# Three turns of adding rows back, moved to between the halves of the next item's gate and up

## The reference

```python
for e in range(N_EXPERTS):                      # 32 experts, D_EXPERT = 512
    hdn = jax.nn.silu(xn @ w_gate[e]) * (xn @ w_up[e])
    out = out + combine[:, e:e + 1] * (hdn @ w_down[e])
return x + out.reshape(bsz, t, d)
```

## Time and profile before

| | |
|---|---|
| runs, us | 833.37, 835.3, 836.32; median 835.3 |
| the profiled execution, us | 835.14, of which span 833.4 |
| granted TensorE clock, mean | 0.979 |
| PE busy | 771.5 us, 93% |
| DVE, ACT, POOL busy | 429.3, 320.9, 262.5 us |
| matmuls of the item loop: gate and up L1718, down L1747, gather L1677, turns L1706 | 169.1, 94.2, 70.5, 52.9 us |
| chain that ended last | PE 59%, DMA 17%, DVE 12%, SyncE's queue 7% |
| DMA in the item loop | 422 GB/s, busy share about 1.0 |

### The profile page before, as it was taken

How to read it: one execution, slowest core, us unless ns; L and a number is a source line. 1 busy time by engine, 2 the same in 40 slices (tenths; PEclk the granted TensorE clock), 3 DMA queues, 4 the chain that set the end, 5 groups by cost and what they waited for, 6 DMA issues and landing times.

```text
span 833.4 us, 21585 instructions
## 1 busy us (share of the span) xinstructions
PE 771.5 (93%) x8619; PEld 589.2 (71%) x8620; DVE 429.3 (52%) x1168; ACT 320.9 (39%) x556; POOL 262.5 (31%) x134
## 2 busy tenths in 40 slices
PE   4999999999999999999999979999998879989964
PEld 4999999999999999875556545555555545545532
DVE  3156978899994334064443433444443334434424
ACT  5433767555335844162223222322332213323223
POOL 4846699978576778400000000000000000000001
PEclk9999999999999999999999988999999999999997
DMA  7734343424444835986899999999999999999993
GB/s 251 236 106 148 102 141 113 153 96 144 154 170 152 302 125 207 340 344 232 361 421 422 422 422 422 422 422 422 422 422 422 422 422 422 422 422 422 423 422 142
DMA packets 53943, 250.77 MB, mean 301 GB/s; under 512 B 6713, under 2 KB 6731, under 8 KB 29333
## 3 DMA queue, kind: packets, MB, share of 16 engines
q1 hardware_dynamic: 50496, 247.74, 75.2%
q10 hardware_dynamic: 3413, 2.58, 1.2%
HBM read 247.54 MB, written 2.76 MB: 300 GB/s over the span
## 4 chain that ended last, share of the span: by engine, by line
PE 59%; DMA 17%; DVE 12%; SPq 7%; ACT 2%; issue 2%; ACTq 1%; DVEq 0%
PE bank L1571 24%; DMA piece<-in_exp_w_up 16%; PE bank L1718 12%; DVE bank L1097 7%; PE bank L1747 6%; SPq L566 6%; PE bank L1677 4%; PE bank L1706 4%; PE bank L1569 4%; DVE sq L1159 1%; PE bank L1734 1%; PE bank L1684 1%; DMA stage<-in_norm_g 1%; ACT cvb L845 1%; ACT w_hi L763 0%
## 5 line engine op out<-in xcount | busy, mean ns | idle before, releaser
L633 POOL TENSOR_TENSOR w_lo<-raw,w_hi 128x2048 fp32r<-128x2048 f32 x39 | 180.4, 4629 | 62.3 <-ACT w_hi L763 62.2
L1718 PE MATMUL bank<-piece,xe 128*32 128x256 f32 x2816 | 169.1, 392 | 29.0 <-DMA piece<-in_exp_w_up 23.2
L1718 PEld LDWEIGHTS bank<-piece,xe 128*32 128x32 f32 x2816 | 97.1, 113 | 93.6 <-issue 42.9
L1571 PE MATMUL bank<-x_hi,w_hi 128*128 128x384 f32 x432 | 145.6, 337 | 0.3 <-DVE ua L1116 0.2
L1571 PE MATMUL bank<-x_hi,w_lo 128*128 128x384 f32 x432 | 144.6, 335 | 0.0
L1571 PE MATMUL bank<-x_lo,w_hi 128*128 128x384 f32 x432 | 144.6, 335 | 0.0
L694 POOL TENSOR_SCALAR n_out<-n_out,small 128x512 f32<-128x512 f32 x2 | 3.6, 1786 | 442.2 <-DVE small L1456 442.2
L1097 DVE SCALAR_TENSOR_TENSOR bank<-ub,vec,bank 128x256 f32<-128x256 f32 (+1 forms) x416 | 137.2, 418 | 0.0
L763 ACT ACTIVATE w_hi<-raw 128x2048 fp32r<-128x2048 f32 x39 | 74.8, 1919 | 74.8 <-PE bank L1571 71.2
L1747 PE MATMUL bank<-piece,hidT 128*32 128x256 f32 x1408 | 94.2, 384 | 5.5
L1416 DVE SCALAR_TENSOR_TENSOR silu_and_hid<-bank,few,silu_and_hid 64x256 f32<-64x256 f32 x44 | 21.5, 488 | 132.8 <-ACT silu_and_hid L953 132.8
(11 more groups left out here) (239 smaller groups left out, 1020.8 us busy)
## 6 DMA issues: line engine op xcount, KB each, us to landing
piece<-in_exp_w_down SPq DMA_DIRECT2D x64, 1024.0 KB, 26.7
piece<-in_exp_w_gate SPq DMA_DIRECT2D x64, 1024.0 KB, 26.2
piece<-in_exp_w_up SPq DMA_DIRECT2D x64, 1024.0 KB, 26.6
raw<-in_w_in SPq DMA_DIRECT2D x28, 1024.0 KB, 5.2
raw<-in_w_out_a SPq DMA_DIRECT2D x4, 1024.0 KB, 5.1
raw<-in_w_out_b SPq DMA_DIRECT2D x4, 1024.0 KB, 5.2
raw<-in_w_o SPq DMA_DIRECT2D x4, 1024.0 KB, 5.0
out<-n_out SPq DMA_DIRECT2D x6, 256.0 KB, 2.2
```

Of the source, the lines that this page charges most:

```text
L633: pool.tensor_tensor(w_lo[u % NW][:, :, :], raw[u % NW][:, :, :], w_hi[u % NW][:, :, :].bitcast(F32), ALU.subtract).then_inc(lo_ready, 1)
L1571: ins = pe.matmul(b, wp[:, k % UK, cols], xp[:, k, :], start=start, stop=stop)
L1718: last = pe.matmul(GU[q * T:(q + 1) * T, :], xe[:, k, :], wide(pairs[q // 2], k)[:, q % 2 * QE:(q % 2 + 1) * QE], start=(k == 0), stop=(k ...
```

## The change

All three turns of an item's addition now stand between the two halves of the next item's gate and up, with the waits that the first turn needs ahead of them. The wait for `y_ready` moves with them from in front of `gather()`. None is left behind the gather, behind the row transposes or between the halves of down. What a turn computes, the other engines' lists and SyncE's list are unchanged.

```diff
@@ item(), TensorE @@
                     last.then_inc(done, 1)
+                    if part == 0:
+                        pe.wait_ge(y_ready, i + 2)
+                        pe.wait_ge(back_ready, i + 1)
+                        for turn in range(NT):
+                            pe.wait_ge(combined, i * NT + (turn + 1))
+                            combine(turn)
 
                 pe.wait_ge(picked, i + 2)
-                pe.wait_ge(y_ready, i + 2)
                 gather()
-                pe.wait_ge(back_ready, i + 1)
-                pe.wait_ge(combined, i * NT + 1)
-                combine(0)
                 pe.wait_ge(consts, 11)
                 pe.wait_ge(hid_ready, i + 1)
...
                 turn_rows()
-                pe.wait_ge(combined, i * NT + 2)
-                combine(1)
                 pe.wait_ge(hidT_ready, i + 1)
...
                     last.then_inc(done, 1)
-                    if part == 0:
-                        pe.wait_ge(combined, i * NT + 3)
-                        combine(2)
```

## The result

The changed kernel took 841.29 us (median of its runs, 840.07 to 842.35) against 835.81 for the kernel before (833.37 to 836.54): ratio 1.0069, interval 1.0051 to 1.0087. It is slower by some 5.5 us; 843.0 was predicted. Its profiled execution took 842.35 us, with a span of 840.6 against 833.4.

The account below looks back on a forecast made before the run. Weights bound the kernel before, TensorE the changed one: item 0 (+1.9 us), 42 items of 9.99 and 7 boundaries of 1.0 end the last down 7.9 us later, so 835.14 + 7.9 = 843.0 us, range 837.0 to 848.5.

Parts of the forecast that it names:

- What bounds: Item loop: weights set the end before the change; TensorE has 36 us of slack, 0.82 us for each item.
- Removed and added: Each item on TensorE: 0.76 us removed at the turns' old places, 1.75 added between the halves; item 9.99 us.
- Item 0: First item of the loop: its turns wait for GpSimd's zeroing of back_to, so the next item starts 1.9 us later.
- Boundaries: Seven round boundaries in the item loop: each adds 1.0 us on TensorE, as in the kernel before.
- The stream of weights: SyncE's refills restart 3.9 us later; the last up piece lands at 815.6, 6.6 us before TensorE asks for it.
- The slow clock: Item loop: low clock follows waits for pieces and goes with them; some 9 us, part of the 36 us.
- A: Item loop: an item grows by under about 0.82 us, weights stay the bound, 836 to 837.6 us; chance 0.15.
- B: Item loop: more small stalls; another 0.1 us per item gives 847 us, over 848.5 from +1.12; chance 0.11.

## Why the prediction came out as it did

**What bounds.** Right, and it is the step that carried it: weights before, TensorE after, slack 36 us or 0.82 an item. The halved refills show both sides.

**Removed and added.** Right, each term within 0.03 us: gate and up with turns 5.21 (predicted 3.45 + 1.75 = 5.20), gather to down 3.05 (3.06), down 1.72 (1.75), item 9.98 (9.99). That turn 1 would bring back nothing and turn 0 only 0.18, since the row copy is late next, shows in the wait for `rows_of_x` in 44 items. One side sum was off: with a drain of 0.166 for 0.14 the forecast would move by 2.2 us for the two waits between turns (3.4 with the entry), not by 2.5. The turns kept their 0.58.

**Item 0.** The mechanism was right, the size within 0.2 us where the clock stayed up (11.04 and 11.15); in the profiled execution (13.24) a later zeroing added 0.6 us and the low clock 1.5, which I hadn't expected behind a stall of 1.7 us.

**Boundaries.** The mis-sized term. I carried 1.0 us over from the kernel before; it is 0.66 at the first one (434.30 to 444.94 is 10.64, less 9.98) and 0.62 in the mean of all seven, together 2.7 us too much. This is most of why 843.0 lies above 841.3. The last item should start at 818.7 and started at 818.00:

```profile
818.00 1.94 PE L1718 MATMUL bank<-piece,xe 128*32 128x256 f32 x32
...
821.46 1.93 PE L1718 MATMUL bank<-piece,xe 128*32 128x256 f32 x32
```

It was 0.17 later at the loop's start, 2.1 later in item 0, 2.7 earlier at boundaries and 0.3 earlier in 42 items. That the profiled execution lies only 0.7 us below the forecast is in part luck: two errors of opposite sign, item 0 and the boundaries, met in it.

**The stream of weights.** Right in direction. Restarted later by the longer items 0 to 2, the refill of the earlier trace rows came at 416.46 (414.2 predicted, item 0 being the difference), and the last up piece was issued at 792.05 for 785.67:

```profile
416.46 0.34 SPq L566 DMA_DIRECT2D piece<-in_exp_w_gate  x1
...
792.05 2.08 SPq L566 DMA_DIRECT2D piece<-in_exp_w_up  x1
```

If it took 26 us to land as in the earlier trace rows, that was at about 818, an estimate; TensorE asked at 821.46. The margin was 3.4 us instead of 6.6, still a margin.

**The slow clock.** Right that it goes with the waits. The 9 us put on it were too few: of the 36 us, 23.2 are waits and about 0.2 behind each of the ten is restart (item 26 took 2.79 more than 9.01 for a wait of 2.59), which leaves about 11, an estimate. No term of the sum rests on it.

**Rivals.** A didn't occur with three turns, but it is just what happens with two. B's clock did not swing: with some six short idles in a period it stayed at 1.00 from 500 to 820 us. The Trainium skill, "TensorE: Matmul & The Clock Gate", section "A second HAM failure mode: psum-queue depth-cycling", warns of frequent short idles between groups of matmuls. This trace shows no such swing.

## To carry to other kernels

When one resource is full and another has slack, divide the slack by the number of times the edited code runs: 36 us over 44 items, 0.82 us. An edit that costs less is free (within the 0.3% that runs can tell), one that costs more is paid at the full rate for the rest. And before work is moved, ask what it covers where it stands: three turns cost 0.76 us there and 1.75 between the halves, since two of them lay under a copy and under VectorE.

## What was not expected of the hardware

The clock fell behind a stall of 1.69 us in item 0 (granted 0.59 over the 2.91 us of the half behind it), while a stall of 1.72 us in the kernel with one turn there left it up, and in the kernel before a wait of 2.59 us (gate and up of item 26, first row below) was followed by a half at full speed, one of 2.66 us (item 36, second row) by one that was not:

```profile
632.93 1.93 PE L1718 MATMUL bank<-piece,xe 128*32 128x256 f32 x32 [2.59 <-DMA piece<-in_exp_w_up]
...
737.31 3.10 PE L1718 MATMUL bank<-piece,xe 128*32 128x256 f32 x28 [2.66 <-DMA piece<-in_exp_w_up]
```

The length of one wait doesn't tell whether the clock falls to its lower level. In item 0 the fall cost 1.5 us.

A turn costs 0.58 for matmuls worth 0.44, whether it stands behind plain matmuls or behind another turn. A round boundary's cost on TensorE went with how many matmuls of down stand in a row ahead of it: 0.45 us of idle with 32, 0.84 with 16.
